# Running sums of the gates: broadcast by DMA from DRAM instead of by matmul (hybrid GLA, DeltaNet and MLA block)

## What is computed

```python
def gdn_chunk_scan(q, k, v, g, beta, s0):
    ...
    g_cum = jnp.cumsum(g, axis=2)
    g_h = jnp.swapaxes(g_cum, 2, 3)
    diff = g_h[..., :, None] - g_h[..., None, :]
    decay = jnp.where(incl, jnp.exp(jnp.where(incl, diff, 0.0)), 0.0)
    k_beta = k * beta[..., None]
    l_strict = jnp.where(strict, jnp.einsum('bnthd,bnshd->bnhts', k_beta, k) * decay, 0.0)
    t_inv = lax.linalg.triangular_solve(eye + l_strict, ...)
    ...
    att = jnp.where(incl, jnp.einsum('bnthd,bnshd->bnhts', q, k) * decay, 0.0)
```

## Time and profile before

| what | value |
|---|---|
| median of 3 runs | 2805.42 us |
| lowest, highest | 2805.41, 2808.85 us |
| the profiled execution's own time | 2797.98 us |
| its span in the trace | 2796.2 us |
| mean granted clock of TensorE | 0.942 of full |
| PE busy / DVE / ACT / POOL | 86% / 38% / 27% / 25% |

### The profile page before, as it was taken

How to read it: one execution, slowest core, us unless ns; L and a number is a source line. 1 busy time by engine, 2 the same in 40 slices (tenths; PEclk the granted TensorE clock), 3 DMA queues, 4 the chain that set the end, 5 groups by cost and what they waited for, 6 DMA issues and landing times. The chain is left out here.

```text
span 2796.2 us, 31490 instructions
## 1 busy us (share of the span) xinstructions
PE 2417.8 (86%) x10714; PEld 1593.8 (57%) x10714; DVE 1052.5 (38%) x2357; ACT 755.8 (27%) x1971; POOL 696.4 (25%) x1149
## 2 busy tenths in 40 slices
PE   6999987887977787999999999998767975789998
PEld 3565555463645466555474446665454754666677
DVE  1133235646564232433321122235745662233321
ACT  1112033313141132444321111214313231234421
POOL 1000000878575500000000000000788678100000
PEclk9999999999999899999999999999889997899999
DMA  7112311211212101111121231123212221031333
GB/s 253 55 60 91 123 61 57 62 43 58 57 59 57 48 25 49 48 60 47 61 76 60 92 106 60 46 63 106 74 38 80 80 65 48 15 115 62 107 108 133
DMA packets 210248, 203.39 MB, mean 73 GB/s; under 512 B 30218, under 2 KB 203758, under 8 KB 209582
## 3 DMA queue, kind: packets, MB, share of 16 engines
q1 hardware_dynamic: 204910, 180.26, 20.9%
q0 software_dynamic: 5184, 21.12, 2.2%
HBM read 184.51 MB, written 16.85 MB: 72 GB/s over the span
## 5 line engine op out<-in xcount | busy, mean ns | idle before, releaser
L965 PE MATMUL bank<-hT,ring 128*128 128x512 f32 (+2 forms) x1824 | 714.9, 534 | 13.4 <-DVE hT L1628 7.1
L965 PE MATMUL bank<-WORK 128*128 128x128 f32 (+7 forms) x2896 | 477.0, 326 | 220.8 <-DVE WORK L1881 183.4
L965 PEld LDWEIGHTS bank<-WORK 128*128 128x128 f32 (+4 forms) x2896 | 349.5, 191 | 358.8 <-issue 329.1
L965 PE MATMUL bank<-ring,hT 128*128 128x256 f32 (+3 forms) x2240 | 487.4, 374 | 31.2 <-DMA ring<-in_w_in_dram 14.3
L965 PEld LDWEIGHTS bank<-hT,ring 128*128 128x128 f32 (+1 forms) x1824 | 336.1, 191 | 300.1 <-issue 265.3
L965 PEld LDWEIGHTS bank<-ring,hT 128*128 128x128 f32 x2240 | 407.0, 197 | 115.2 <-issue 46.2
L923 POOL TENSOR_TENSOR WORK<-WORK 32x31 f32<-32x31 f32 (+15 forms) x496 | 293.4, 592 | 38.9
L921 POOL TENSOR_TENSOR WORK<-WORK 32x31 f32<-32x31 f32 (+15 forms) x496 | 279.2, 563 | 38.9
L965 PE MATMUL bank<-yT,ring 128*128 128x512 f32 (+1 forms) x768 | 276.4, 494 | 0.0
L953 POOL DMA_DIRECT2D yT<-xs x2 | 1.1, 566 | 991.0 <-PE bank L965 991.0
L965 PEld LDWEIGHTS bank<-yT,ring 128*128 128x128 f32 x768 | 139.2, 192 | 86.0 <-issue 76.7
(11 more groups left out here) (186 smaller groups left out, 2275.2 us busy)
## 6 DMA issues: line engine op xcount, KB each, us to landing
ring<-in_w_in_dram SPq DMA_DIRECT2D x92, 1024.0 KB, 5.4
ring<-in_ada_w_dram SPq DMA_DIRECT2D x24, 1024.0 KB, 6.5
ring<-in_w_branch_dram SPq DMA_DIRECT2D x24, 1024.0 KB, 5.0
LD<-WORK SPq DMA_DIRECT2D x64, 128.0 KB, 2.0
WORK<-XD POOLq DMA_DIRECT2D x64, 128.0 KB, 2.7
ring<-in_w_out_dram SPq DMA_DIRECT2D x8, 1024.0 KB, 5.0
ring<-in_mla_q_up_dram SPq DMA_DIRECT2D x8, 576.0 KB, 4.6
xs<-yT POOLq DMA_DIRECT2D x2, 2048.0 KB, 9.9
```

What stands on the lines that cost most here:

```text
L965: return nc.tensor.matmul(o, a, b, start=start, stop=stop, skip_group_check=True)
```

## The change

Once a layer, `dg` now also forms the running sums as rows: 8 matmuls of 8 columns of gates with the triangles into a third bank, two more copies on ACT to `GT` (8 partitions each, in the space of `bKE`), and two more writes by SP to a new DRAM tensor `GD`. The signal on which SP and DVE wait is now given by the last of the three copies.

`d1` has no part on PE any more and takes no bank. A new item `dc`, SP's alone, brings two rows of `GD` for each direction into `DC`, each broadcast to all 128 partitions: 2 DMAs an item, 128 KB each, 64 in all. SP waits there for the writes of `GD`, for `d2` of the tile that used the half of `DC` before, and for `dy6` of the group before on PE (a wait that DVE had in `d1`). DVE's four operations of `d1` read `DC` instead of a bank and write it in place, after waiting for the DMAs.

In the head, the order `d1, d2, dt, d3` becomes `dc, d3, d1, d2, dt`.

```diff
@@ -212,7 +212,7 @@
...
-        one, two = ([(k, l, g, 2 * p + i) for k in ("d1", "d2", "dt", "d3")] for i in range(2))
+        one, two = ([(k, l, g, 2 * p + i) for k in ("dc", "d3", "d1", "d2", "dt")] for i in range(2))
...
@@ -317,13 +317,13 @@
...
-         "dt": 0, "db": 0, "sol": 0, "dv": 0, "dg": 2}
+         "dc": 0, "d1": 0, "dt": 0, "db": 0, "sol": 0, "dv": 0, "dg": 3}
...
@@ -459,6 +459,7 @@
...
+        GD = nc.dram_tensor("GD", (DEPTH, 2, BH, T), F32, kind="Internal").ap()
...
@@ -506,6 +507,7 @@
...
+        GT = bKE[:, 0, :]
...
@@ -856,6 +860,20 @@
...
+                    for r in range(2):
+                        sp.dma_start(GD[l, r], GT[r * CH:r * CH + BH, :]).then_inc(s_gc, 16)
+                elif u[0] == "dc":
+                    _, l, g, tt = u
+                    i = tt % 2
+                    sp.wait_ge(s_gc, 32 * (l + 1))
+                    p = plan_prev_tile(u)
+                    if p:
+                        sp.wait_ge(*done(("d2",) + p[1:], "dve"))
+                    if g:
+                        sp.wait_ge(*done(("dy6", l, g - 1, tt), "pe"))
+                    for r in range(2):
+                        sp.dma_start(DC[:, i, r * 256:(r + 1) * 256].rearrange("p (u n) -> p u n", u=2),
+                                     GD[l, r, 2 * g:2 * g + 2, tt * P:(tt + 1) * P].partition_broadcast(P)).then_inc(s_dc[i], 16)
...
@@ -1129,20 +1147,15 @@
...
-                        ins = tr(psum(it, 1)[0:16, tt * P:(tt + 1) * P],
-                                 BETA[:, tt, :])
+                        tr(psum(it, 1)[0:16, tt * P:(tt + 1) * P], BETA[:, tt, :])
+                    for tt in range(TT):
+                        for r in range(2):
+                            ins = mm(psum(it, 2)[r * CH:r * CH + BH, tt * P:(tt + 1) * P], GG[:, tt, r * BH:(r + 1) * BH],
+                                     kc(C_TRI + r * P))
                 elif k == "dn":
                     pe.wait_ge(*done(("dnq",) + it[1:], "act"))
                     a0 = q0 if it[3] < 2 else 0
                     ins = mm(ps[:, a0:T], ONES[:, :], bSQ[:, a0:T])
-                elif k == "d1":
-                    _, l, g, tt = it
-                    pe.wait_ge(*done(("dg", l), "dve"))
-                    for r in range(2):
-                        for hh in range(2):
-                            u = 2 * r + hh
-                            ins = mm(ps[:, u * P:(u + 1) * P],
-                                     col(GG, tt, g, u).broadcast_to([P, P]), kc(C_TRI + r * P))
...
@@ -1446,7 +1459,9 @@
...
-                    nc.scalar.activation(BT, psum(it, 1)[0:16, :].rearrange("p (t n) -> p t n", t=TT), ACT.Copy).then_inc(
+                    nc.scalar.activation(BT, psum(it, 1)[0:16, :].rearrange("p (t n) -> p t n", t=TT), ACT.Copy)
+                    nc.scalar.activation(GT[0:BH, :], psum(it, 2)[0:BH, :], ACT.Copy)
+                    nc.scalar.activation(GT[CH:CH + BH, :], psum(it, 2)[CH:CH + BH, :], ACT.Copy).then_inc(
                         signal(it, "act", "bt"), 1)
...
@@ -1837,12 +1852,11 @@
...
                     _, l, g, tt = it
-                    if g:
-                        dve.wait_ge(*done(("dy6", l, g - 1, tt), "pe"))
                     dve.wait_ge(*done(("dg", l), "dve"))
+                    dve.wait_ge(s_dc[tt % 2], 32 * (2 * rounds(l, g) + tt // 2 + 1))
                     for u in range(4):
                         c = slice(u * P, (u + 1) * P)
-                        ins = V_.scalar_tensor_tensor(DC[:, tt % 2, c], ps[:, c], col(GC, tt, g, u), kc(C_NEG + (u // 2) * P),
+                        ins = V_.scalar_tensor_tensor(DC[:, tt % 2, c], DC[:, tt % 2, c], col(GC, tt, g, u), kc(C_NEG + (u // 2) * P),
                                                       ALU.subtract, ALU.min)
...
@@ -1868,6 +1882,7 @@
...
+                    dve.wait_ge(s_gc, 32 * (l + 1))
```

More of the change, by code:

```diff
@@ L605, in hybrid_block @@
         s_xzero = stack.enter_context(nc.semaphore("x_dram_zeroed"))
+        s_gc = stack.enter_context(nc.semaphore("decay_rows_out"))
+        s_dc = [stack.enter_context(nc.semaphore(f"decay_in{i}")) for i in range(2)]
         s_beta = stack.enter_context(nc.semaphore("beta_rows_out"))
@@ L657, in hybrid_block @@
                 continue
-            if k not in ("nh", "cv", "dsilu", "dsil2", "dnq", "z2", "rstd", "dt", "db", "sol", "dv"):
+            if k not in ("nh", "cv", "dsilu", "dsil2", "dnq", "z2", "rstd", "d1", "dc", "dt", "db", "sol", "dv"):
                 parts["pe"].add(k)
@@ L842, in _ @@
             todo = [(where[last_use[replaced[u]]] if u in replaced else -1, 0, n, u) for n, u in enumerate(units)]
-            todo += [(where[it], 1, 0, it) for it in plan if it[0] in ("dg", "dt", "db")]
+            todo += [(where[it], 1, 0, it) for it in plan if it[0] in ("dg", "dc", "dt", "db")]
             for _, scratch, _, u in sorted(todo, key=lambda t: t[:3]):
```

6 lines of the change are left out of this document (3 added, 3 removed), and 2 rows, old and new, of the table PHASE.

## The result

The changed kernel takes **2823.8 us** (median of 6 runs, 2816.6 to 2834.2), beside 2805.1 for the kernel before in the same rounds: ratio 1.0075, 95% interval 1.0047 to 1.0103, some 21 us slower. The sign is the one forecast and the time lies at the very end of the range, but the forecast was +9.2; more than half of the loss is missing from the sum. The profiled execution is the longest of the changed kernel's, 2834.2 us with a span of 2832.3, so its rows show more of the loss than the median has.

What follows compares the result with a forecast made beforehand. Prediction took the path to be mostly PE, leaving it for DRAM, POOL's solves and VectorE; -7.2 + 2.7 + 5.4 + 4.8 + 3.5 = +9.2 on 2805.4 gave 2815 us; case's own range 2811 to 2821, 8 in 10 2799 to 2824.

Steps and rivals of the forecast that it cites:

- The first head, +5.4: First head of each layer: `d3`'s 1.42 us before `dt` plus one 1.27 us wait for ACT; range 0 to +9.
- Matmuls removed, -7.2: Bodies 1 and 3, where the path runs along PE: four pairs at 1.8 us each arrive earlier; body 2 gains 0.
- `dg`, +4.8: Narrow matmuls and two more ACT copies delay VectorE's copy: 3.0 us in layer 0, 1.8 in layer 1; range 0 to 6.
- POOL beside VectorE, +3.5: Solves on the path: `d1` with two SBUF inputs slows POOL by 0.87 us a pair, two pairs a layer.
- The head in body 4, +2.7: Before the `LD` write: `d3` adds 1.4 us in layer 1, 0 in layer 0; slower `d1` adds 1.3 over both.
- The broadcasts, 0: Broadcasts land in 2.7 us, just hidden in body 4; the first head's late second pair is hidden by slack.
- PE's 18.88 and 5.44 us before body 1: PE's waits in layers 1 and 0, taken as slack hiding the first head's second-pair broadcasts, some 4 us late.
- body 2's 1.3: Possible loss in body 2 if its slower `d1` shows, counted in the upper end of the forecast's range.
- PE's gain coming through: Rival: PE is the bound; pairs of bodies 1 to 4 pay 14.4, `dg` costs 3.6: -10.8, 2794.6 us; 15%.
- No change: Rival: POOL and `d1` not slowed, first heads cost only `d3`, `dg` only PE's time: +0.6, 2806 us; 30%.
- The late broadcasts: Rival: from about 4.6 us landing, broadcasts miss body 4; at 7.0, first heads 4 late each: +13, 2828 us; 13%.

Runs made afterwards that it cites:

- the hybrid: The change in the old order, but with matmuls instead of broadcasts for the second pair of each first head; 0.9969 of the kernel before, -9 us.

## Why the prediction was right and wrong

**The first head, +5.4: the step that failed.** I walked the head item by item with the output branch's items where they stood, and added `d3`'s 1.42 and one wait of 1.27 us. For `d3` first that is right in layer 1 (2.9 us) and low in layer 0 (5.1), where PE's transposes are waited for as well. What the sum lacked is the weave: `head` returns ten items for a pair's two tiles instead of eight, and every list woven with it is dealt out anew. That costs 3.5 us in layer 0's head and 2.4 and 3.9 us on the way from `dg` to the heads. Measured in the changed kernel, from the copy in `dg` to the first transpose: 10.3 us in layer 0 and 6.8 in layer 1, **17** against 5.4, and above the 9 I gave as the upper end. A kernel in which nothing was added but an idle item showed it at +11 us.

**Matmuls removed, -7.2.** Neither confirmed nor refuted. In the old order they are worth 11.8 us, give or take 5. In the order of the change their removal brought 0.6, give or take 10, which doesn't exclude the 7.2. I had priced removal and order as if they added: +19 for the order and -7 for the rest of the change in the old order would make +12, and the changed kernel has +21. That gap of 9 has an interval of 9 to either side, so it is barely shown that the two don't add, and why they don't stays open. One part is seen in PE's waits for VectorE's transposes before bodies 3 and 5, added over both layers: 7.0 us in the changed kernel and 2.7 with the matmuls put back, 4.6 and 1.0 in the old order. Before body 3 of layer 1 it is 3.02 instead of the 1.25 of the earlier trace rows, the 1.8 that I had said body 2 would wait out. But these waits grow by about 4 us in both orders, so they don't tell the orders apart.

**`dg`, +4.8.** Right in place and, within the interval, in size: 2.2 us of longer wait in layer 0, where I had 3.0, and 1.8 in layer 1 as forecast; +7 (4 to 9) as a kernel of its own.

**POOL beside VectorE, +3.5.** Wrong in who pays. The last but one solve holds such a pair in both layers, and takes 39.85 and 39.94 us from its first operation to its write, against 39.81 and 39.83 before: 0.04 and 0.11 longer, where I had put 0.87 each. POOL's busy time is 695.0 us, against 696.4. VectorE pays instead. In the solves of the bodies the median of `d1` is 706 to 790 ns, 2.1 to 2.3 times the 343 of before and not 1.24 times; in the first solves, right after the stall, it is 464 and 434. All 128 together are 24.4 us longer. What of that reaches the end no run separates. The first solve is shorter where VectorE stands for broadcasts (46.4 and 47.0 us to its write, against 48.8 and 49.7), and the second longer, by 2.5 and 1.0; in the hybrid, without the stall, they are 49.2 and 49.8, and the second 0.6 and 0.1 longer than before. The Trainium skill, in GPSIMD Engine Reference, section 1, Specifications, has POOL and VectorE contend when a VectorE instruction has two SBUF inputs. The `d1` rows agree with it: 333 to 351 ns everywhere with one input in a bank, over 700 in the solves with both in SBUF.

**The head in body 4, +2.7.** A little low, and made of other parts. From the start of the last operation ahead of the head (L1929 before, L1944 after) to the first transpose of `dt` it is 6.59 us instead of 4.61 in layer 1, and 9.35 instead of 7.84 in layer 0: +2.0 and +1.5, together 3.5. None of it is a slower `d1`, for which I had put 1.3: POOL is idle there, and the pair takes 2.18 us, against 2.16. It is `d3` and the wait for its transposes on PE, 0.59 us in layer 1 and 1.73 in layer 0, that I had left out.

```profile
2314.94 1.12 DVE L1944 SCALAR_TENSOR_TENSOR WORK<-WORK,bank 128x128 f32<-128x128 f32 x4 [4.68 <-PE bank L983]
2316.65 1.42 DVE L1889 TENSOR_TENSOR WORK<-bank,WORK 128x256 f32<-128x256 f32 x4 [0.59 <-PE bank L986]
2317.99 2.18 DVE L1859 SCALAR_TENSOR_TENSOR SQ<-SQ,WORK,K 128x128 f32<-128x128 f32 x8
...
2321.53 0.76 DVE L1880 STREAM_TRANSPOSE WORK<-WORK 128x256 f32<-128x256 f32 x2
```

The change in the old order takes 6.20 and 4.58 us for the same stretches: there layer 0 gains 1.6 us, about the 1.48 that `d1` no longer waits for PE. How much of either arrives at the next solve is open; from the last but two to the last but one solve of layer 1 the changed kernel is 7.6 us longer than before, the one with earlier broadcasts 5.2 shorter, and the kernel with only `dg`'s part, whose code there is that of before, 3.6 longer. No broadcast was waited for, as predicted.

**The broadcasts, 0.** They land in 4.6 us, not 2.7, just at the point from which I had said that the rival decides. Its price came from body 4, where nothing waited, and from first heads late by 4 us. In body 4 of layer 1 they even took 5.5 to 7.0 us, and weren't late: I had let them wait 5.2 us for the weight load ahead of them, but they were issued at 2306.60, 0.5 us behind that load's issue, and `d1` began at 2317.99. In the first heads they were late by 6.5, and my reason why that is hidden, PE's 18.88 and 5.44 us before body 1, looked at the wrong wait: body 0 of layer 0 waits for VectorE's own projection work. The result, 0, held all the same as far as can be measured (-7 us with the late pair, -9 without), since the delay was given back later.

**The range.** Its upper end doesn't follow from its own terms. The first head's 9 instead of 5.4 and body 2's 1.3, which was already the figure for both layers, make 2819.5 and not 2821.

**The rivals.** PE's gain coming through (2794.6) is near what the change in the old order does, 2791.0 in the median beside 2798.3, and the 11.8 us of the matmuls there hold both its 14.4 and my 7.2. It was a fair picture of the removal and the wrong one of the change. No change (2806) failed on the first heads. The late broadcasts (2828) come nearest in time, by luck: their mechanism is wrong.

## What to carry over

Where a schedule is made by weaving lists evenly, an item that costs nothing still moves everything it is woven with: count how the lists grow, and look at which other items come to stand on the path, even far ahead of the edit. When a change has an order and an operation in it, try the operation in the old order first; here it was worth -7 us, and the order that was to hide its transfers cost 19. When an operation is priced, split its rows by what runs beside them: the median of 400 ns for `d1` stood for operations of 343 and of over 700. And before calling a delay hidden, find the wait that its own successors end in, on their engine, not the largest wait nearby.

## What was not expected of the hardware

A broadcast of 128 KB to all partitions out of DRAM takes 4.6 us from issue to landing in the median, against 2.0 and 2.7 for plain transfers of 128 KB. An operation of VectorE with its input moved from a bank to SBUF kept its 343 ns while POOL was idle and took 706 to 790 while POOL solved, and POOL's solves of 39.8 us stayed as long as they were. A delay of 7.5 us at one solve was gone at the next, and 64 us with unchanged code differed by 3.6 us between profiles, so a stretch of one profile says little of the end. The rows at 1932.48 and 1934.97 above are the other thing: after a wait of 2.42 us the granted clock fell, and the same matmuls took 1.43 and 1.55 times as long. The profile of the changed kernel has a mean granted clock of 0.932 and that of before 0.942, which goes with PE being as busy with 112 matmuls fewer. But the change in the old order has 0.936 in the median, against 0.942 beside it, and is the faster one, so a lower mean alone does not make a kernel slower; whether the clock has a part in the loss no run here separates.
